# Moving two groups of on-chip buffers by 32 and 160 bytes in a fused hybrid SSD / pooling layer

## The reference, cut to what matters

```python
x = x + 0.5 * swiglu(rms_norm(x, ffn1_norm), ffn1_w_gate, ffn1_w_up, ffn1_w_down)   # width 2816
h = rms_norm(x, mix_norm)
z, xbc, dt_raw, u = split(h @ w_in)
y_ssd  = ssd_group(z, xbc, dt_raw, ...)        # causal conv, chunked scan, 16 heads, gate, norm
y_pool = multiscale_pool_group(u, pool_w, pool_scale)
x = x + concatenate([y_ssd, y_pool], -1) @ w_out
x = x + 0.5 * swiglu(rms_norm(x, ffn2_norm), ffn2_w_gate, ffn2_w_up, ffn2_w_down)
return rms_norm(x, final_norm)
```

## Time and profile before

| | |
|---|---|
| time, median of 2 runs | 1041.89 us (1041.59 to 1042.2) |
| the profiled execution, its own time | 1042.32 us |
| its span (first to last instruction) | 1040.6 us |
| TensorE matmul busy | 1031.2 us, 99% |
| weight loads busy | 847.3 us, 81% |
| VectorE, ScalarE, GpSimd busy | 559.6, 380.4, 179.1 us |
| mean granted TensorE clock | 0.997 of 2.4 GHz |

### The profile page before, as it was taken

The page is one execution under the profiler, slowest core; times in us unless marked ns, Lnnn a source line. Parts: engine busy times, 40 slices in busy tenths (PEclk is TensorE's granted clock), DMA queues, the critical chain, the costliest instruction groups (busy, mean ns, idle before and its releaser), DMA issues.

```text
span 1040.6 us, 13577 instructions
## 1 busy us (share of the span) xinstructions
PE 1031.2 (99%) x4798; PEld 847.3 (81%) x4798; DVE 559.6 (54%) x686; ACT 380.4 (37%) x489; POOL 179.1 (17%) x166
## 2 busy tenths in 40 slices
PE   9999999999999999999999999999999999999997
PEld 7888888888888878878787888888888888888887
DVE  5544444444344468786799795554444444433432
ACT  6433223322333337652234753432333223332332
POOL 1110110101001032221063451110101101101100
PEclk9999999999999999999999999999999999999998
DMA  6533323322333343222222233333333332233222
GB/s 184 150 113 101 101 86 95 101 83 68 99 98 96 101 124 100 82 81 70 73 81 81 62 101 101 101 101 90 92 101 101 96 87 89 79 109 95 86 68 81
DMA packets 188873, 99.09 MB, mean 95 GB/s; under 512 B 3780, under 2 KB 188200, under 8 KB 188840
## 3 DMA queue, kind: packets, MB, share of 16 engines
q1 hardware_dynamic: 188168, 97.60, 32.3%
q10 hardware_dynamic: 672, 1.05, 0.3%
HBM read 96.54 MB, written 2.10 MB: 95 GB/s over the span
## 4 chain that ended last, share of the span: by engine, by line
PE 96%; DVE 3%; issue 1%; ACT 1%; POOL 0%; ACTq 0%; POOLq 0%
PE bank L1150 29%; PE bank L1152 29%; PE bank L1151 29%; PE bank L1222 1%; PE bank L1216 1%; PE bank L1219 1%; PE bank L1471 1%; PE bank L1284 0%; PE bank L1306 0%; PE bank L1472 0%; PE bank L1473 0%; PE bank L1274 0%; DVE w_lo_part L743 0%; DVE ebuf L903 0%; PE bank L1190 0%
## 5 line engine op out<-in xcount | busy, mean ns | idle before, releaser
L1150 PE MATMUL bank<-xghi,w_hi_part 128*128 128x512 f32 x960 | 377.4, 393 | 0.0
L1152 PE MATMUL bank<-xghi,w_lo_part 128*128 128x512 f32 x960 | 373.8, 389 | 0.0
L1151 PE MATMUL bank<-xglo,w_hi_part 128*128 128x512 f32 x960 | 373.6, 389 | 0.0
L743 DVE TENSOR_TENSOR w_lo_part<-w_raw,w_hi_part 128x1024 fp32r<-128x1024 f32 x194 | 253.9, 1309 | 192.8 <-ACT w_hi_part L498 187.5
L498 ACT ACTIVATE w_hi_part<-w_raw 128x1024 fp32r<-128x1024 f32 x194 | 203.8, 1051 | 196.2 <-PE bank L1152 194.7
L1150 PEld LDWEIGHTS bank<-xghi,w_hi_part 128*128 128x128 f32 x960 | 180.2, 188 | 39.9 <-issue 2.8
L1151 PEld LDWEIGHTS bank<-xglo,w_hi_part 128*128 128x128 f32 x960 | 180.3, 188 | 38.4 <-issue 1.2
L1152 PEld LDWEIGHTS bank<-xghi,w_lo_part 128*128 128x128 f32 x960 | 180.2, 188 | 37.5
L1150 PE MATMUL bank<-acthi,w_hi_part 128*128 128x512 f32 x330 | 130.5, 396 | 0.0
L410 POOL TENSOR_TENSOR gate_buf<-gate_buf,rstd 128x512 f32<-128x512 f32 x44 | 57.1, 1298 | 424.5 <-ACT gate_buf L521 424.5
L1152 PE MATMUL bank<-acthi,w_lo_part 128*128 128x512 f32 x330 | 129.4, 392 | 0.0
(11 more groups left out here) (223 smaller groups left out, 805.0 us busy)
## 6 DMA issues: line engine op xcount, KB each, us to landing
w_raw<-in_ffn_w_gate SPq DMA_DIRECT2D x42, 512.0 KB, 3.8
w_raw<-in_ffn_w_up SPq DMA_DIRECT2D x42, 512.0 KB, 3.8
w_raw<-in_w_in SPq DMA_DIRECT2D x29, 512.0 KB, 3.8
w_raw<-in_ffn_w_down SPq DMA_DIRECT2D x32, 384.0 KB, 3.2
w_raw<-in_ffn_w_down SPq DMA_DIRECT2D x32, 320.0 KB, 3.0
w_raw<-in_w_out SPq DMA_DIRECT2D x16, 512.0 KB, 3.6
out<-xtok SPq DMA_DIRECT2D x4, 512.0 KB, 3.4
xload<-in_x SPq DMA_DIRECT2D x3, 512.0 KB, 7.0
```

The costliest lines, as they stand in the source:

```text
L743: dve.tensor_tensor(wlo[:, slot(m)], raw[:, slot(m)], whi[:, slot(m)].bitcast(F32), ALU.subtract).then_inc(w_lo, 1)
L1150: pe.matmul(bank, w, h, start=first and n == 0, stop=False)
L1151: pe.matmul(bank, w, l, start=False, stop=False)
L1152: mm = pe.matmul(bank, wl, h, start=False, stop=last and n == blocks - 1)
```

## The change

A padding tensor is put between `xT` and `xghi`, and the start of the shared region is computed modulo 256 instead of being rounded up to 64.

```diff
+LANES = 256
+WEIGHT_LANE = 128
...
         xT = sb("xT", [P, DK * S])
+        def start_at(residue):
+
+            lane = (residue - nc.sbuf_base) % LANES
+            if lane:
+                sb(f"lane{nc.sbuf_base}", [P, lane // 4])
+
+        start_at(WEIGHT_LANE + 32)
         xghi = sb("xghi", [P, DK * S], F32R)
...
-        base = (nc.sbuf_base + 63) // 64 * 64
+        base = nc.sbuf_base + (WEIGHT_LANE - 32 - nc.sbuf_base) % LANES
```

## The result

The changed kernel takes 1065.13 us (median of 2 runs, 1065.12 to 1065.14) against 1041.89 us. The ratio is 1.0221, with a 95% interval of 1.0205 to 1.0238: 23.2 us slower, outside the range that was given.

The account below looks back on a forecast made before the run. The prediction took TensorE as the bound: number of matmuls times the distance between their starts. 1042.3 + 3.3 - 1.4 = 1044.2 us, with the median 0.4 us lower, gave 1044 us; range 1010 to 1058 us.

Parts of the forecast that it names:

- (a): Norm outputs, moved from distance 0 to +32 bytes: 1.1 ns more on each of 2976 matmuls, +3.3 us.
- (b): Shared region, moved from distance +64 to -32 bytes: 1.1 ns less on each of 1230 matmuls, -1.4 us.
- Term (c): Bounds for both kinds of matmul: at worst the unsettled 231.7 ns, +18.3 us; below, -2.7 us, or -59 us at 213.3 ns.
- slower rival: Gate/up and input stages: both kinds of matmul settle at 233.3 ns, costing 25.4 us, 1067 us; chance 0.13.
- room for a gain: Faster rival, both kinds of matmul: distance drops a step to 220.0 ns, gaining 30.9 us, 1011 us; chance 0.30.
- The rival that nothing happens: All stages: the 2.2 ns come from PSUM banks or other traffic, not the address; 1042 us, chance 0.20.
- (d): VectorE, ScalarE and GpSimd on the moved buffers: covered by idle time, costed at 0, 1 us either way.
- (e): DMA loads of `xload` at the start and stores from `xtok` at the end: unchanged, taken as 0.

## Why the prediction was wrong

**The bound was right.** The time was the number of matmuls times the distance of their starts: 2976 and 1230 matmuls explain the result within 2.5 us.

**The step that failed is the size of terms (a) and (b).** "Halfway between them is 227.8 ns" took the time to be a smooth function of the distance and put a value between the only two known, 0 and 64. The runs give 226.7, 231.7, 233.3 and 228.9 ns at 0, 16, 32 and 64: it is not monotonic, and the middle is worse than both ends. Term (b) also took -32 to lie between 0 and +64, and -32 gives 233.3 ns. Term (a) was +3.3 us and measured +17.4 alone; term (b) was -1.4 and measured +5.6, with the other sign. The prediction had named the reading that would refute it, a gate/up distance outside 225 to 231 ns, and 233.3 is outside.

**The bound above was too low.** Term (c) took 231.7 ns, "the worst that rows show over several matmuls", as the upper bound, +18.3 us or 1060; the range that was stated ended at 1058. A state in which the stream was seen passing is no bound for one in which it can stay; a settled 233.3 ns lay above it, and 1065 us above both. The argument against the slower rival, that the stream leaves such rates within six matmuls, came from a row at distance 0, where the low rate is the one it settles into.

**The slower rival was this case.** It named the place, the rate (one 6.67 ns step up, 35 steps instead of 34) and 1067 us against 1065.13 measured, with a chance of 0.13. The step itself was an estimate from a grid of 6.67 ns per matmul. Six of the nine distances of the map fit it (226.7 and 233.3 ns) and the other three do not (228.9, 231.7 and 234.3), so that +32 and -32 both cost one whole step is measured, but no run explains it. The two rates of before should have been read as "the norm matmuls already sit at the better one", with most of the matmuls to lose from any move; instead the surplus of 13.4 ns was read as room for a gain, with 0.30. No distance tried goes below 226.7 ns.

**The rival that nothing happens** put the 2.2 ns down to what the stages do otherwise; the run with the two distances exchanged refutes that. It also had a rule behind it, of the Trainium skill, SBUF — State Buffer, section "Who interferes with whom": independent read ports for the two operands, and TensorE waits on nobody. Read as "the addresses can't matter", that rule disagrees with the pair with everything moved and the weights moved alone: 226.7 against 233.2 ns for the same instructions, by nothing but where the weights lie relative to the data. The measurement decides. The isolated gap of 215.8 ns for 512 columns, from the Trainium skill, TensorE: Matmul & The Clock Gate, section "Back-to-back issue gap", does not describe this stream either: no float32r matmul here settles below 226.7.

**Terms (d) and (e) were right.** Busy time of the other engines moved by 0.5 us at most, the conversions kept their durations (1311 and 1052 ns against 1309 and 1051), and the DMAs their 7.0 and 3.4 us to landing.

**What stays open.** It is shown that the time is set by the start of the moving data relative to that of the weights, for each kind of matmul by itself, and that the load that runs beside a matmul is the one that lengthens it most (the run with the low weights alone moved). That 256 is the period is shown only for +64. How the memory or the array makes this is open: shorter loads made the stream slower or left it as it was (at +64 with half loads, at +32 with quarter loads), and never faster, so a count of collisions with the loaded bytes does not explain it. Open as well is why a matmul grows whose neighbour alone is out of step, and what the 13.4 ns over the columns' own time are, which stay even at distance 0.

## What to carry to other kernels

When TensorE runs back to back in float32r, read the distance from start to start of settled matmuls for each pair of tensors, and compare stages: a difference of a few ns for the same instruction can be an address effect; in this kernel the slowest placement costs 2.5% more than the fastest (1066.08 against 1040.35 us). For this shape, let the weights and all moving tensors begin at the same remainder modulo 256, the best of the nine distances tried, and check the addresses again whenever a small tensor is inserted ahead of them. Don't interpolate between two such readings; each distance has to be run.

## What the runs showed of the hardware

- A 512-column float32r matmul settles at 226.7 ns (distance 0), 228.9 (+64), 231.7 (+16), 234.3 (-96) or 233.3 (the others tried), at a granted clock of 0.997 to 0.999 of 2.4 GHz.
- Shifting weights and data together by 32 bytes changes nothing (1042.21 against 1042.38 us).
- +64 and -64 differ (228.9 and 233.3 ns), and +128 is about as bad as +32 (233.3 ns, in some stretches 232.1).
- With the low weights alone 32 bytes on, the next start after the matmul beside which they are loaded comes after 238.6 ns instead of 227.1, and after their own matmul after 228.3 instead of 226.8.
- Matmuls with shorter loads, and so fewer output rows, are never faster. With 64 columns in two of three loads they take 229.4 ns at distance 0 instead of 226.7, and 228.8 at +64 as before; with 32 columns in most groups 230.7 and 230.2 ns (1048.66 and 1054.51 us against 1042.2 for the kernel).
